# One layer kernel: mended front, key projections from unnormed x, scores in four quadrants of TensorE

## The reference, cut to what matters

```python
h = rms_norm(x, norm_mix_g)                 # x: 256 tokens x 1024
proj = h @ w_in                             # 1024 x 2048: s5 | r | k | v, 512 columns each
y_s5 = s5_mixer(proj[:, :512], ...)         # diagonal state space, 32 groups
y_rw = rwkv7_mixer(h, r, k, v, ...)         # 8 heads of 64; token shifts, three LoRA gates
#   kk = k * k_k per head, divided by max(sqrt(sum kk^2), 1e-12)
x = x + concat(y_s5, y_rw) @ w_out
x = x + moe_ffn(rms_norm(x, norm_moe_g))    # router, top 4 of 32, gate/up/down of 1024 x 1024
x = x + per_layer_embedding(...)            # small
out = rms_norm(x, final_norm_g)
```

## Time and profile before

| | us |
|---|---|
| median of 3 runs | 1209.95 (1209.51 to 1210.59) |
| profiled execution, its own time | 1203.81 |
| its span, first to last instruction | 1202.0 |
| PE busy | 1076.2 (90%) |
| DVE / ACT busy | 365.5 (30%) / 176.3 (15%) |
| mean granted TensorE clock | 0.991 |
| HBM read | 428.70 MB |

### The profile page before, as it was taken

One profiled execution on the slowest core, in us unless ns is written; L12 is line 12 of the kernel. 1 busy time (PEld: TensorE's weight loads), 2 busy tenths in 40 slices (PEclk: granted clock), 3 DMA queues, 4 the chain that ended last, 5 costly groups with the idle time before them and its releaser, 6 DMA issues. The chain is left out here.

```text
span 1202.0 us, 18872 instructions
## 1 busy us (share of the span) xinstructions
PE 1076.2 (90%) x8132; PEld 492.5 (41%) x8132; DVE 365.5 (30%) x739; ACT 176.3 (15%) x288; POOL 17.5 (1%) x18
## 2 busy tenths in 40 slices
PE   6989998899999988888888888888888888888896
PEld 5779884443334333333333333333333333333342
DVE  5997925522222111111222111111111221211122
ACT  5580231400000000000000000000000000000023
POOL 0000005000000000000000000000000000000000
PEclk9989999899999999999999999999999999999999
DMA  9301184589999999999999999999999999999970
GB/s 324 125 2 37 43 328 142 211 359 426 428 428 430 428 429 428 427 428 429 429 429 430 428 429 428 428 428 430 429 429 428 429 428 428 427 430 428 430 289 35
DMA packets 44531, 430.28 MB, mean 358 GB/s; under 512 B 4912, under 2 KB 15536, under 8 KB 19920
## 3 DMA queue, kind: packets, MB, share of 16 engines
q1 hardware_dynamic: 44304, 429.24, 85.5%
q0 software_dynamic: 192, 0.52, 0.1%
HBM read 428.70 MB, written 1.05 MB: 358 GB/s over the span
## 5 line engine op out<-in xcount | busy, mean ns | idle before, releaser
L1221 PE MATMUL bank<-arena 128*64 128x512 f32 (+5 forms) x5136 | 847.3, 467 | 91.0 <-DMA arena<-in_exp_w_up 58.3
L1221 PEld LDWEIGHTS bank<-arena 128*64 128x64 f32 (+4 forms) x5136 | 307.8, 128 | 607.0 <-issue 446.2
L239 PE MATMUL bank<-arena 64*64 64x64 f32 (+7 forms) x2048 | 161.6, 264 | 15.4 <-ACT arena L362 8.5
L239 PEld LDWEIGHTS bank<-arena 64*64 64x64 f32 (+3 forms) x2048 | 129.3, 144 | 45.7 <-issue 26.3
L1410 ACT ACTIVATE arena<-arena 128x512 f32<-128x512 f32 x32 | 20.1, 630 | 520.2 <-DVE arena L1458 520.2
L1463 DVE TENSOR_SCALAR arena<-bank 128x512 f32<-128x512 f32 x32 | 22.1, 691 | 227.7 <-PE bank L1221 227.7
L1473 DVE COPY arena<-bank 128x512 f32<-128x512 f32 x32 | 22.1, 691 | 202.8 <-PE bank L1221 202.8
L1458 DVE TENSOR_SCALAR arena<-bank 128x512 f32<-128x512 f32 x32 | 22.1, 691 | 194.0 <-PE bank L1221 194.0
L1413 ACT ACTIVATE arena<-bank 128x256 f32<-128x256 f32 x32 | 12.3, 383 | 326.2 <-PE bank L1517 326.2
L1434 DVE TENSOR_TENSOR arena<-bank,par 128x512 f32<-128x512 f32 x33 | 22.8, 691 | 77.9 <-PE bank L1221 77.9
L1466 DVE SCALAR_TENSOR_TENSOR arena<-arena 128x512 f32<-128x512 f32 x32 | 33.7, 1052 | 1.1
(11 more groups left out here) (275 smaller groups left out, 406.7 us busy)
## 6 DMA issues: line engine op xcount, KB each, us to landing
arena<-in_exp_w_gate SPq DMA_DIRECT2D x64, 2048.0 KB, 32.2
arena<-in_exp_w_down SPq DMA_DIRECT2D x64, 2048.0 KB, 35.4
arena<-in_exp_w_up SPq DMA_DIRECT2D x64, 2048.0 KB, 35.3
arena<-in_w_in SPq DMA_DIRECT2D x8, 1024.0 KB, 12.9
arena<-in_w_out SPq DMA_DIRECT2D x4, 1024.0 KB, 6.3
arena<-in_ple_w_gate SPq DMA_DIRECT2D x2, 2048.0 KB, 33.4
arena<-in_xT SPq DMA_DIRECT2D x1, 1024.0 KB, 6.0
arena<-in_lora SPq DMA_DIRECT2D x1, 1024.0 KB, 13.6
```

Of the source, the lines that this page charges most:

```text
L239: return nc.tensor.matmul(out, lhsT, rhs, start=start, stop=stop, skip_group_check=True)
L1221: return nc.tensor.matmul(out, lhsT, rhs, start=start, stop=stop, skip_group_check=True)
```

## The change

- **Start.** x times the norm's gain (`x_gain`) is made before the root is known; `project(0)` and `project(1)`, the keys, take it, and DVE multiplies by the inverse root while it copies them out (`copy_normed`), between the LoRA mixes. `hT` is one instruction in place of eight. 20 small matmuls run on PE ahead of the sum of squares. `con` is loaded behind the LoRA weights.
- **Keys.** Half of each token shift of k and v goes to ACT (`rest_of_shift`), half stays on DVE (`add_shifted`). Two memsets of `EL` and the zeroing of `taps` go to POOL. The head norms are summed into 16 columns, rooted and inverted there, and spread again by 16 matmuls; the root and the reciprocal over 128 x 1024 go.
- **Order.** `turn_g` is split in two around `project(4)`, `stack_u` and `into` stand elsewhere, ACT's copies are reordered.
- **Scores.** Units 8 to 15 are written crosswise (`cross`), so that the two `pair`s issued together lie in all four quadrants; the same for `turn`. ACT copies three of the five scores unmasked, DVE masks two of them in the last levels. `s5_out(3)` and the head sums of `rk` move. In the recurrence the crosswise units need `first_half` waits.
- **Router block.** `gatesT` is built in four row groups of 32 and the bias matmuls use one each; `exp_b_down` is loaded in four parts; four small matmuls before the gates, five before the gather; `router_b` is loaded in the front block.
- In the expert loop two semaphores become one.

```diff
@@ DVE, start
+                dve.wait_ge(s["xT_in"], 16)
+                for k in range(KD):
+                    ts(x_gain[:, k, :], xT[:, k, :], prm("g_mix")[:, k:k + 1], None, ALU.mult).then_inc(s["x_scaled"], 1)
+                def copy_normed(n):
+                    dve.wait_ge(s["proj_done"], n + 1)
+                    tt(raw["k"][:, 2 * n:2 * n + 2, :], banks[n][:, :].rearrange("p (f t) -> p f t", t=T),
+                       root[:, None, :].to_broadcast([P, 2, T]), ALU.mult).then_inc(s["proj_copied"], 1)
                 dve.wait_ge(s["rms_root"], 1)
                 link(V.reciprocal(root, root))
-                for k in range(KD):
-                    stt(hT[:, k, :], xT[:, k, :], prm("g_mix")[:, k:k + 1], root, ALU.mult, ALU.mult).then_inc(s["h_ready"], 1)
+                tt(hT[:, :, :], x_gain[:, :, :], root[:, None, :].to_broadcast([P, KD, T]), ALU.mult).then_inc(s["h_ready"], 1)
...
+                for n, (dst, mu) in enumerate(((xw, "mu_w"), (xa, "mu_a"), (xg, "mu_g"))):
+                    if n:
+                        copy_normed(n - 1)
@@ PE, start
+                for _ in range(20):
+                    mm(banks[0][:, 0:P], ones_early, ones_early, True, True)
...
-                            last = mm(banks[n % 2][:, f * T:(f + 1) * T], win[q][:, k, f * P:(f + 1) * P], hT[:, k, :], k == 0, k == KD - 1)
+                            last = mm(banks[n % 2][:, f * T:(f + 1) * T], win[q][:, k, f * P:(f + 1) * P], (hT if n > 1 else x_gain)[:, k, :], k == 0, k == KD - 1)
@@ DVE, head norms
-                dve.wait_ge(s["kk_root"], 1)
-                link(ts(kb, kb, 1e-12, None, ALU.max))
-                link(V.reciprocal(kb, kb))
-                link(tt(kkn, kkn, kb, ALU.mult))
+                dve.wait_ge(s["kk_summed"], 2)
+                for b in range(2):
+                    d = kkn[:, 2 * b:2 * b + 2, :]
+                    last = tt(d, d, banks[6 + b].rearrange("p (f t) -> p f t", t=T), ALU.mult)
@@ PE, middle
-                head_sums(kksq, 4).then_inc(s["kk_summed"], 1)
+                for n in range(4 * TT):
+                    tok = slice(n // FT * P, (n // FT + 1) * P)
+                    last = mm(banks[6][:, 2 * n:2 * n + 2], kksq[:, n % FT, tok], head_pair, True, True)
+                last.then_inc(s["kk_summed"], 1)
+                turn_g(0)
                 project(4)
+                pe.wait_ge(s["kk_norm"], 2)
+                for n in range(4 * TT):
+                    tile, f = n // FT, n % FT
+                    for h in range(2):
+                        last = mm(banks[6 + f // 2][h * CH:(h + 1) * CH, (f % 2) * T + tile * P:(f % 2) * T + (tile + 1) * P],
+                                  norms[:, 2 * n + h:2 * n + h + 1].to_broadcast([P, CH]), ident, True, True)
+                last.then_inc(s["kk_summed"], 1)
+                turn_g(1)
                 project(5)
+                stack_u()
+                pe.wait_ge(s["kk_norm"], 3)
                 kernel_taps()
-                turn_g()
-                stack_u()
                 into(0)
                 into(1)
@@ PE, scores
-                        for u in range(8 * b, 8 * b + 8):
-                            last = pair(bank[:, (u % 8) * CH:(u % 8 + 1) * CH], fm(l, u), fm(r, u))
+                    for u in range(8):
+                        o = slice(u * CH, (u + 1) * CH)
+                        ins = pair(banks[bank][:, o], fm(l, u), fm(r, u))
+                        if u == 7:
+                            ins.then_inc(s["scores_done"], 1)
+                        last = pair(banks[bank + 1][:, o], fm(l, u + 8), fm(r, u + 8), cross=True)
+                    last.then_inc(s["scores_done"], 1)
@@ ACT, scores
+                for m, dst in ((1, Mx), (3, RB), (4, RK)):
+                    for b in range(2):
+                        act.wait_ge(s["scores_done"], 2 * m + b + 1)
+                        A(dst[:, 8 * b:8 * b + 8, :], banks[SCORE_BANK[m] + b].rearrange("p (u t) -> p u t", t=CH), ACT.Copy).then_inc(s["scores_moved"], 1)
@@ PE, recurrence (c >= 2 is cross)
+                    if cross:
+                        pe.wait_ge(s["first_half"], 3 * c - 4)
@@ PE, router block
+            for _ in range(4):
+                mm(banks[7][:, 0:P], ident, ident, True, True)
             pe.wait_ge(s["gates_ready"], 1)
-            for tile in range(TT):
-                last = nc.tensor.transpose(banks[5][0:E, tile * P:(tile + 1) * P], gates[:, tile, :], ident)
+            rows = [slice(n * E, (n + 1) * E) for n in range(4)]
+            for n in range(4):
+                last = mm(banks[5][rows[n], 0:P], gates[:, n // 2, :], ident, True, True)
...
-                mm(banks[n][:, :], gatesT[:, n // 2 * P:(n // 2 + 1) * P], bias_down[:, n % 2 * HF:(n % 2 + 1) * HF], True, False)
+                mm(banks[n][:, :], gatesT[rows[n], :], bias_down[rows[n], :], True, False)
@@ PE, expert block, before the first gather
+            for _ in range(5):
+                mm(YB[:, 0:P], ident, ident, True, True)
```

More of the change, by code:

```diff
@@ L239, in mm, with pair @@
             return nc.tensor.matmul(out, lhsT, rhs, start=start, stop=stop, skip_group_check=True)
-        def pair(out, lhsT, rhs, start=True, stop=True):
+        def pair(out, lhsT, rhs, start=True, stop=True, cross=False):
             for h in range(2):
-                a = slice(h * CH, (h + 1) * CH)
-                last = mm(out[a], lhsT[a], rhs[a], start, stop)
+                a, o = slice(h * CH, (h + 1) * CH), slice((h ^ cross) * CH, (h ^ cross) * CH + CH)
+                last = mm(out[o], lhsT[a], rhs[a], start, stop)
             return last
@@ L412, in lora_out, with copy_g, rest_of_shift @@
                             last.then_inc(s["lora2_copied"], 1)
-                copy_proj(0)
-                copy_proj(1)
+                def copy_g(n):
+                    m, q = n // 4, n % 4
+                    act.wait_ge(s["g_turned"], n + 1)
+                    A(gturn[m][:, 4 * q:4 * q + 4, :], banks[2 + q].rearrange("p (j q) -> p j q", q=P), ACT.Copy).then_inc(s["g_copied"], 1)
+                def rest_of_shift(m, src, dst, signal):
+                    act.wait_ge(s["eps_ready"], 2)
+                    for i in range(FT):
+                        last = A(dst[:, i, :], src[:, i, :], ACT.Copy, scale=rest_mu[:, m, i:i + 1])
+                    last.then_inc(s[signal], 1)
+                act.wait_ge(s["proj_done"], 1)
+                clear(9, 1)
                 act.wait_ge(s["lora1_done"], 1)
@@ L421, in _ @@
                 lora_out(0)
-                act.wait_ge(s["pads_clear"], 4)
-                for m in range(2):
-                    act.wait_ge(s["g_built"], m + 1)
-                    for g in range(2):
-                        a, o = half(g)
-                        A(gpad[m][a, :, :, o].rearrange("p j n c -> p n j c"), gprod[m][a], ACT.Copy).then_inc(s["g_padded"], 1)
                 lora_out(1)
@@ L430, in _ @@
                 A(kksq[:, :, :], kkn[:, :, :], ACT.Square).then_inc(s["kk_squared"], 1)
+                act.wait_ge(s["pads_clear"], 7)
+                for m in range(2):
+                    act.wait_ge(s["built"], m + 1)
+                    for g in range(2):
+                        a, o = half(g)
+                        A(gpad[m][a, :, :, o].rearrange("p j n c -> p n j c"), gprod[m][a], ACT.Copy).then_inc(s["padded"], 1)
+                act.wait_ge(s["proj_copied"], 2)
                 copy_proj(2)
                 lora_out(2)
+                act.wait_ge(s["kk_summed"], 1)
+                A(norms, banks[6][:, 0:4 * TT * 2], ACT.Sqrt).then_inc(s["kk_norm"], 1)
+                for m in range(2):
+                    for g in range(2):
+                        a, o = half(g)
+                        A(gfirst[a, m, :, o], gprod[m][a, 0], ACT.Copy).then_inc(s["padded"], 1)
                 act.wait_ge(s["decay_ready"], 1)
@@ new lines, in _ @@
+                for b in range(2):
+                    dve.wait_ge(s["scores_done"], b + 1)
+                    d = X[:, 8 * b:8 * b + 8, :]
+                    link(tt(d, banks[SCORE_BANK[0] + b].rearrange("p (u t) -> p u t", t=CH), col(C_SU1), ALU.mult))
+                    link(tt(d, d, eye, ALU.add))
+                    turn_x(b).then_inc(s["scores_copied"], 1)
+                for b in range(2):
+                    dve.wait_ge(s["scores_moved"], b + 1)
+                    level_mask(0, b)
@@ L1029, in turn @@
                     pe.wait_ge(s["scaled"], 4)
[L1030 to L1035 removed]
+                    if n:
+                        pe.wait_ge(s["turned"], 2 * n)
+                    arr, eye = (bh, kh, vv)[n], con[:, C_ID2:C_ID2 + CH]
+                    for u in range(8):
+                        o = slice(u * CH, (u + 1) * CH)
+                        ins = pair(banks[0][:, o], fm(arr, u), eye)
+                        if u == 7:
+                            ins.then_inc(s["turn_done"], 1)
```

(6 more changed lines are left out.)

278 lines of the change are left out of this document (151 added, 127 removed).

## The result

| | us |
|---|---|
| after, median of 7 runs | 1199.51 (1196.54 to 1209.53) |
| before, median of the 7 runs beside them | 1209.51 (1204.73 to 1210.59) |
| ratio after / before | 0.9941, 95% interval 0.9914 to 0.9968 |
| profiled execution after: span | 1199.4 |
| PE / DVE / ACT busy | 1077.2 / 361.5 / 182.6 |

The change is faster, by 7 us by the ratio (4 to 10), where 17.4 were forecast. The runs of the changed kernel are spread over 13 us; the slowest has a mean granted clock of 0.983, the fastest one of 0.993.

The account below looks back on a forecast made before the run. The first refill of the expert weight slots was taken to set the end. Gains of 8.5 + 4.9 - 0.5 + 4.5 = 17.4 us off 1209.95 gave 1192.6, say 1193 us, range 1189 to 1202.

Parts of the forecast that it names:

- What bounds the kernel: Whole kernel: every microsecond by which the first refill comes sooner comes off the end one for one.
- start, to the head sums: Kernel start to the keys' head sums: these start at 53.1 instead of 56.76, 3.7 us sooner, ACT being last.
- middle, to the first mask: Head sums to scores: waits and half-clock time removed, some matmuls added; 4.8 us gained.
- scores and levels, to the gelu: Scores to gelu: four quadrants save 0.85 us per group and masked copies leave the path; 4.9 us gained.
- recurrence and output, to the router block: Gelu to router block: same matmuls plus five PE waits, DVE and ACT work unchanged, POOL's split hidden; 0.5 us lost.
- router block, to the refill: Router block and first gather: overlapping bias matmuls and a faster gather, capped by the stream; 4.5 us gained.
- I take 11.9: Front: the sum of squares ends and PE's first projection starts at 11.9 us, 5.0 us sooner.
- 8.5 in all: Kernel start to the scores: they start at 101.0 instead of 109.54, 8.5 us sooner.
- The cap by the stream: First refill: the eight slots land at 243.8, 6.0 before 249.8, limiting the router block's gain, taken as 4.5 us.
- The refill gains little: Rival, router block: small matmuls only delay and clock stays 0.50, 2 us instead of 4.5; 1195.5 us, chance 0.09.
- No change that counts: Rival: something late, such as the output projection waiting for weights, eats the faster front's gain; chance 0.02.
- Slower: Rival: granted clock falls after PE idles, each fall costing about 3 us; eight falls give 1217 us, chance 0.04.

Follow-up runs that it names:

- number 8: Changed kernel with expert biases loaded early, two output weights loaded late, a semaphore per key weight, s5_out(0) ahead of the fourth score; 1186.68 us, ratio 0.9827.
- number 1: The changed kernel run again without any edit, as control; 1198.74 us, ratio 0.9927 to the kernel before.
- edit 6: Changed kernel with two of the four 1 MB output-projection weight loads issued later, at the S5 wait; 1197.25 us, ratio 0.9922.
- 2: Changed kernel with the expert-bias transfers issued early, ahead of the wait for s5_out_done; 1194.31 us, ratio 0.9893.
- 5: Kernel before the change, with only the expert-bias transfers issued early; 1209.89 us, ratio 1.0005.
- number 7: Changed kernel with a separate semaphore for each of the two key weights; 1196.79 us, ratio 0.9922.
- 11: number 8 with crosswise placing off, both pairs in the same two corners; 1190.01 us, ratio 0.9858.
- 4: Changed kernel with crosswise placing off, both pairs in the same two corners; 1201.37 us, ratio 0.9944.
- number 9: Kernel before the change, with only the router part: gatesT and bias_down in four row groups, nine small matmuls; 1201.35 us, ratio 0.9958.
- 3: Changed kernel with s5_out(0) moved from level 0 to ahead of the fourth score; 1198.84 us, ratio 0.9929.
- 12: number 8 without the nine small matmuls in the router block and ahead of the first gather; 1191.59 us, ratio 0.9877.

## Why the prediction was wrong

**What bounds the kernel** was right: the first refill, one for one (three kernels leave 953.4 to 953.6 us from refill to end of span: before, after and number 8). The terms, as gains in us against the profile of before:

| term | forecast | after | after, again (1) | mended (8) |
|---|---|---|---|---|
| start, to the head sums | 3.7 | 0.1 | 0.3 | 3.7 |
| middle, to the first mask | 4.8 | 3.5 | 5.0 | 3.0 |
| scores and levels, to the gelu | 4.9 | -0.1 | 0.8 | 4.9 |
| recurrence and output, to the router block | -0.5 | -6.6 | -6.6 | 0.9 |
| router block, to the refill | 4.5 | 5.7 | 5.7 | 5.7 |
| sum | 17.4 | 2.6 | 5.2 | 18.2 |

Three terms fail in both profiles of the changed kernel: the output, the scores and the start. The profiles make the miss look larger than it is. That of before was of a fast execution (1203.81 against a median of 1209.95), those of after were not (1201.14 against 1199.51, and 1198.6 against 1198.74), while the prediction took the gap of 6.1 to be the same on both sides. By the ratios the change gives 7 to 9 us of the 17.4.

The front can give the forecast gain: number 8, the same code with three stalls removed and one product moved, meets 230.37 against the forecast 231.2. That it fits so closely is in part luck: its middle is 1.8 short, and the output stage and the router block give 2.6 more than forecast. What failed is that I worked out how long the work takes and left out what else moves when it is done sooner.

**The output stage: the step that failed.** "DVE's and ACT's work is the same ... POOL's bias split, which ends 20 us before ACT asks for it, are hidden". The split is hidden as far as its result goes, but it was not free: DVE's operations beside it take up to five times as long (5.35 us for 1.11). The trace of before showed it, 3.64 for four records of L808 with 1.11 for the next four, and I looked only for who waits for POOL. The term at nothing measured 6.6 us between gelu and router block (69.44 after, 62.85 before, 61.95 in number 8), and it also swallowed part of what edit 6 gains. That POOL is the cause is shown by 2, where DVE's operations are short again and another one is slowed at POOL's new place, and by 5 and 8. In time, removing it alone is worth 4.1 us of the 17.4 (2). The Trainium skill has a rule for it, "SBUF — State Buffer", SBUF: two separate sides: a DVE operation in a two-port mode, or with two inputs in SBUF while the GpSimd one reads SBUF, and a GpSimd operation share a pair of ports under an exclusive lock, and the loser is blocked outright. By that rule a chain of DVE operations beside POOL is priced at POOL's durations; the trace agrees in kind (L877 and L879 stretch to 5.35 and 2.63 beside POOL operations of 1.0 to 2.1, and the reciprocal L874, with one input, stays at 3.35). That the ports are the reason no run here shows.

**Start, "I take 11.9".** Wrong premise: both key weights are asked for, so 14.51. I had read the landing of one. The term of 3.7 measured 0.1; with its own semaphore it measured 3.7 (number 7). ACT as the last engine at 53 was right.

**To the scores, 8.5 in all.** It measured 3.6, mostly for want of the start. The middle's own 4.8 came out at 3.5 in the first profile and at 5.0 in number 1, so this term was right in size. In both the waits of 4.56 and 0.73 went, and the window of 81 to 85 us has its clock at 1.00 for 0.50. In the first profile `turn_g(0)`, after PE's wait, runs at a lower clock (0.64 from 58 to 62 us; 16 transposes 3.03 us, `project(4)` 7.70 where `project(5)` takes 7.07); in number 1 it doesn't (1.94 and 7.07, clock 1.00). The fall is one execution's.

**Scores and levels, 4.9.** It measured -0.1 (48.21 us from first mask to gelu before, 48.26 after), 0.8 in number 1 (47.44) and 4.9 in number 8 (43.35). The total of 43.3 was met there, its parts less so: the XY add comes 13.7 behind the first mask for 11.9 forecast and the rest takes 29.65 for 31.4, and the moved product shifts time from the second part to the first. 3.1 of the 4.9 are the quadrants (11 against 8). The other 1.8 I put down to the copies off the path; no run isolates it. With two corners the stage takes 47.89 unmended (4), about the 0 gain that the prediction gave for that case, and 46.45 mended (11).

What I missed is that PE can stand without waiting for a result. With PE faster, gaps marked "issue" appear (0.93 to 0.98 us in the scores), and none there with two corners (4); the kernel before has one too, of 1.09 us at 128.5. That moving the two 1 MB loads gives 3.7 us in this stage is shown by 6, as far as one profile of each can; that the loads delay the instructions is argued, and against it stand a gap of 1.23 us in the scores without any load (6) and one of 1.04 us at 82.7, far from any, after the change. What these gaps are stays open.

The rule of the Trainium skill that the prediction weighed, "TensorEngine Tiling (Array Packing)", Restrictions and Gotchas, is that different row tiles cannot access the same PSUM bank at once. It doesn't hold the quadrants back here: two row halves write one bank, and 64 records take 1.16 us for 2.08 in two corners. The 53 ns that the prediction gives one record alone stand in no row; the 17.33 us of 40 records of 512 columns (8) make 54 ns of 64 columns, as an estimate.

**Recurrence, 0.5**: right in size; from gelu to the output projection's first block 36.82 us before, 37.10 after, 37.28 in number 8. **Router block, 4.5**: right; 5.1 by number 9, the refill itself 5.7. The cap by the stream took about 1.3 of that in number 9.

**The rivals.** None of the six was what happened, and none of the three signs of being wrong came: not slow crosswise records, not waits on ACT between 60 and 100, not a pause of the stream. (The price of "The refill gains little" should read 1195.1: 17.4 less 2.5 is 14.9.) "No change that counts" had the kind right, something late that eats the front's gain, but named the output weights, which come in time. "Slower" had half of it: in the first profile the clock is lower behind such waits, 0.55 from 14.5 to 17 us after one of 2.3, 0.72 from 112 to 116 after one of 2.6, and 0.50 from 204.7 to 209 after one of 5.2. Number 6 has a wait of 2.60 at the same place as the second and keeps 1.00. "Nothing in the trace shows falls after waits of 2 to 3 us" held for the earlier trace rows and was too little to lean on.

## What to carry to other kernels

An engine that nobody waits for can still slow another: before a row is called hidden, compare the same operation's duration beside it and apart from it. When a stage is brought forward, list everything whose start doesn't move with it (transfers behind other transfers, shared semaphores, instructions), since the stage will run into them; and if several repairs each give next to nothing, try them together before dropping one, because a later stall can absorb what the others give. Read a wait's number, not only its semaphore: 32 for two transfers is a wait for the later one.

## What the runs showed of the hardware

- Beside POOL's casts and subtractions, four DVE tensor-by-scalar operations took 5.35 us in place of 1.11, and a tensor-tensor operation of 128 x 512 took 2.63 in place of 0.69; a reciprocal of 128 x 512 took 3.35 beside POOL and 3.34 apart from it. Where POOL's work was moved, it slowed the DVE operations there (two in 3.77 us in place of 1.27).
- 64 x 64 float32 tiles in all four quadrants, two row halves writing one bank: 64 records in 1.16 us in number 8 and 62 in 1.10 in number 6 (17.7 to 18.1 ns each), against 64 in 2.08 in two corners in number 11 (32.5 ns; 30.5 in the earlier trace rows).
- PE stood up to 2.68 us with nothing in the profile to release it, there next to a 1 MB load (3). Of the gaps in number 1, those of 0.48, 0.88 and 0.85 us went when the loads were moved and that of 0.93 stayed, at 1.23 (6).
- With nine small matmuls in gaps of 1 to 2 us the granted clock stays at 1.00 up to the refill and router start to refill takes 21.1 us (8); without them the clock is 0.50 from 226 on, and it takes 24.3 (12).
- A wait of PE of 2.6 us was followed by a mean clock of 0.72 to 0.75 in two executions of the changed kernel, and by 1.00 in number 6.
